# Layer norms that measure from a first mean over half of the chunks, in a two-layer Conformer / MLA / expert trunk

## What is computed

```python
def layer_norm(x, g, b):
    mu = jnp.mean(xf, -1, keepdims=True)
    var = jnp.mean(jnp.square(xf - mu), -1, keepdims=True)
    return ((xf - mu) * lax.rsqrt(var + LN_EPS) * g + b).astype(x.dtype)

# norm 0, inside the convolution mixer
y = jax.nn.silu(layer_norm(conv, g_ln, b_ln)) @ w_out
# norms 1 and 3 (mixer), norm 2 (SwiGLU of layer 0)
xp = layer_norm(ALPHA * xp + mp, ln_g[i, 0], ln_b[i, 0])
xp = layer_norm(ALPHA * xp + fp, ln_g[i, 1], ln_b[i, 1])
```

## Time and profile before

| | |
|---|---|
| median of 3 runs | 1913.56 us (1909.77 to 1916.96) |
| profiled execution | 1914.0 us, of which the span is 1912.4 us |
| mean granted TensorE clock | 0.957 |
| busy | TensorE 91%, weight loads 78%, VectorE 73%, ScalarE 58%, GpSimd 5% |
| moved | 460.86 MB, 241 GB/s over the span |

### The profile page before, as it was taken

The page is one execution under the profiler, slowest core; times in us unless marked ns, Lnnn a source line. Parts: engine busy times, 40 slices in busy tenths (PEclk is TensorE's granted clock), DMA queues, the critical chain, the costliest instruction groups (busy, mean ns, idle before and its releaser), DMA issues.

```text
span 1912.4 us, 27003 instructions
## 1 busy us (share of the span) xinstructions
PE 1748.3 (91%) x9480; PEld 1492.9 (78%) x9480; DVE 1388.5 (73%) x1494; ACT 1104.1 (58%) x1144; POOL 86.4 (5%) x174
## 2 busy tenths in 40 slices
PE   6998899998888998779999999989999999999990
PEld 5987899997757887757888888768888888888880
DVE  4995655436455665456888889888888888888885
ACT  4434543226254454136777777667777777777771
POOL 0000000000013441010000000000000000000001
PEclk9999999999889998959999999999999999999995
DMA  9653454443111441047999999989999999999963
GB/s 236 206 183 94 111 154 148 138 121 131 37 52 55 130 117 48 2 152 266 347 348 356 346 358 352 340 337 372 370 376 380 371 371 361 393 370 372 383 246 111
DMA packets 229126, 460.86 MB, mean 241 GB/s; under 512 B 16533, under 2 KB 121652, under 8 KB 229025
## 3 DMA queue, kind: packets, MB, share of 16 engines
q1 hardware_dynamic: 217438, 433.76, 63.5%
q10 hardware_dynamic: 6067, 18.86, 2.8%
q0 software_dynamic: 5536, 7.12, 1.4%
HBM read 441.40 MB, written 18.76 MB: 241 GB/s over the span
## 4 chain that ended last, share of the span: by engine, by line
issue 54%; PE 38%; DVE 4%; ACT 2%; DMA 1%; POOL 1%; SPq 0%; POOLq 0%; ACTq 0%; DVEq 0%
PE ps L1859 7%; PE ps L1861 7%; PE ps L1860 7%; PE ps L2200 3%; PE ps L1924 3%; PE ps L2169 2%; PE ps L1964 1%; PE ps L1957 1%; PE ps L2219 1%; PE ps L2195 1%; PE ps L2220 1%; DMA xtok<-in_x_sample 1%; PE ps L2279 1%; PE ps L2054 0%; DVE rstd L1349 0%
## 5 line engine op out<-in xcount | busy, mean ns | idle before, releaser
L1764 DVE TENSOR_TENSOR w_lo<-raw,w_hi 128x2048 fp32r<-128x2048 f32 x212 | 484.0, 2291 | 82.9 <-ACT w_hi L1145 82.9
L1145 ACT ACTIVATE w_hi<-raw 128x2048 fp32r<-128x2048 f32 x212 | 406.1, 1919 | 161.8 <-PE ps L2407 151.8
L1773 DVE TENSOR_TENSOR w_lo<-raw,f_hi 128x2048 fp32r<-128x2048 f32 x126 | 284.0, 2285 | 27.2 <-PE ps L2311 17.4
L1154 ACT ACTIVATE f_hi<-raw 128x2048 fp32r<-128x2048 f32 x126 | 237.3, 1913 | 70.6 <-PE ps L2311 47.9
L1859 PE MATMUL ps<-x_hi,w_hi 128*128 128x304 f32 x672 | 210.2, 313 | 25.1 <-DVE x_lo L1355 15.0
L2405 PE MATMUL ps<-w_hi,g_hi 128*128 128x512 f32 x560 | 220.1, 393 | 3.3 <-DVE w_lo L1764 3.3
L2407 PE MATMUL ps<-w_hi,g_lo 128*128 128x512 f32 x560 | 218.2, 390 | 0.0
L2406 PE MATMUL ps<-w_lo,g_hi 128*128 128x512 f32 x560 | 218.0, 389 | 0.0
L1861 PE MATMUL ps<-x_lo,w_hi 128*128 128x304 f32 x672 | 206.6, 307 | 0.0
L1860 PE MATMUL ps<-x_hi,w_lo 128*128 128x304 f32 x672 | 206.1, 307 | 0.0
L1274 DVE TENSOR_TENSOR w_lo<-raw,w_hi 128x2048 fp32r<-128x2048 f32 (+4 forms) x129 | 135.5, 1096 | 83.4 <-ACT w_hi L884 83.3
(11 more groups left out here) (412 smaller groups left out, 3107.9 us busy)
## 6 DMA issues: line engine op xcount, KB each, us to landing
raw<-in_moe_w_gu SPq DMA_DIRECT2D x224, 1024.0 KB, 7.1
raw<-in_moe_w_down SPq DMA_DIRECT2D x112, 1024.0 KB, 7.0
raw<-in_ffn_w_gu SPq DMA_DIRECT2D x44, 512.0 KB, 5.0
kvn<-in_cache_ckv SPq DMA_DIRECT2D x128, 128.0 KB, 2.4
raw<-in_conv_w_in SPq DMA_DIRECT2D x16, 512.0 KB, 8.3
raw<-in_ffn_w_down SPq DMA_DIRECT2D x16, 512.0 KB, 4.0
rows_in<-zrow ACTq DMA_DIRECT2D x13, 512.0 KB, 4.9
raw<-in_conv_w_out SPq DMA_DIRECT2D x8, 512.0 KB, 6.7
```

The costliest lines, as they stand in the source:

```text
L1145: nc.scalar.activation(w_hi[:, u % SPLIT], raw[:, u % RAW], ACT.Copy).then_inc(hi_done, 1)
L1154: nc.scalar.activation(first_hi(k), first_raw(k), ACT.Copy).then_inc(hi_done, 1)
L1764: V.tensor_tensor(w_lo[:, u % SPLIT], raw[:, u % RAW], w_hi[:, u % SPLIT].bitcast(F32), ALU.subtract).then_inc(lo_done, 1)
L1773: V.tensor_tensor(w_lo[:, (U_MOE + k) % SPLIT], first_raw(k), first_hi(k).bitcast(F32), ALU.subtract).then_inc(lo_done, 1)
```

## The change

All four norms are made in another way. When half of the chunks are there (0 to 3), their mean is taken as a first mean, and all chunks are stored as distances from it. Squares are taken of these distances. At the end the sum of the distances gives the shift to the true mean (`ln_delta`), and the variance is the mean square minus the shift's square. Each chunk is then re-centred by the shift before it is scaled. So the squares of six chunks are made before the last product has ended.

- VectorE, second to fourth norm (`norm_sums`): after the first and second residual it adds chunks 0 to 3 into `rstd`. After the third it reads the first mean, subtracts it from chunks 0 to 5, adds chunks 4 and 5 into `rstd`, and adds squares 0 to 3 into `sq[:, 0]`. After the fourth residual it subtracts from chunks 6 and 7. Each residual ends with a wait for itself.
- TensorE (`shift_and_spread`): no `mean_terms` between products; one sum after the third product for the first mean; after the fourth, four sums of what VectorE prepared, then chunks 6 and 7 of the mean, then squares 6 and 7.
- ScalarE: six squares after the splits (in the third norm ahead of the split of unit 9 of 12), two at the end; the root reads `rstd` from SBUF, where VectorE has put the variance.
- First norm: four sums of chunks 0 to 3 stand between the convolution's products; VectorE subtracts from chunks 0 to 5 ahead of the last `add_taps`; TensorE makes eight sums after the last taps and the rest as above. The convolution's product groups alternate between two pairs of PSUM banks in place of three. The edge rows are turned after the variance; VectorE copies them after the norm and one split, and ScalarE issues their nine transfers behind two splits.
- GpSimd's `iota` into `place_no` waits for the last scaling of the fourth norm instead of the last product.

```diff
+    HALF_MEAN = 2.0 / D
+    ln_m0 = [rstd[:], gate[:, 0], ln_rows[:, DC - 3], xt[:, 0, 0:T]]
+    ln_banks = [(4, 5), (6, 7), (6, 7), (6, 7)]
...
-        pool.wait_ge(unit_used, U_MOE)
+        pool.wait_ge(ln_scaled, DC * 4)
...
+        def squares(n, chunks):
+
+            for c in chunks:
                 act.wait_ge(ln_cent, DC * n + c + 1)
...
+        def root(n):
+
+            squares(n, (DC - 2, DC - 1))
+            act.wait_ge(ln_ready, ln_base(n + 1))
+            nc.scalar.activation(rstd[:], rstd[:], ACT.Sqrt, bias=eps[:, 0:1]).then_inc(ln_std, 1)
...
         for i in range(12):
+            if i == 9:
+                squares(2, range(DC - 2))
             split(U_DOWN + i + AHEAD)
...
         settle()
+        first_mean(0)
+        distance(0, range(DC - 2))
         add_taps(7)
...
+            def center(c):
+
+                mark(V.tensor_tensor(work[:, c], work[:, c], ln_delta, ALU.subtract))
+                at[c] = n_own[0]
+
+            v.wait_ge(ln_mean, 2 * n + 2)
+            chain(V.tensor_scalar(ln_delta, ps[:, mean_at, 0:T], 1.0 / D, None, ALU.mult))
+            mark(V.tensor_tensor(ln_dsq, ln_delta, ln_delta, ALU.mult))
+            squared = n_own[0]
+            center(0)
+            v.wait_ge(dve, squared)
+            v.wait_ge(ln_var, n + 1)
+            V.scalar_tensor_tensor(out=rstd[:], in0=ps[:, var_at, 0:T], scalar=1.0 / D, in1=ln_dsq,
+                                   op0=ALU.mult, op1=ALU.subtract).then_inc(ln_ready, 1)
+            center(1)
             v.wait_ge(ln_std, n + 1)
             chain(V.reciprocal(rstd[:], rstd[:]))
             for c in range(DC + 2):
                 if c < DC:
+                    v.wait_ge(dve, at[c])
                     V.tensor_tensor(work[:, c], work[:, c], rstd[:], ALU.mult).then_inc(ln_scaled, 1)
+                    if c + 2 < DC:
+                        center(c + 2)
...
+        def norm_sums(n, i):
+
+            if i == 0:
+                mark(V.tensor_tensor(rstd[:], work[:, 0], work[:, 1], ALU.add))
+            elif i == 1:
+                settle()
+                chain(V.tensor_tensor(rstd[:], rstd[:], work[:, 2], ALU.add))
+                V.tensor_tensor(rstd[:], rstd[:], work[:, 3], ALU.add).then_inc(ln_ready, 1)
+            elif i == 2:
+                first_mean(n)
+                distance(n, range(DC - 2))
+                v.wait_ge(ln_cent, DC * n + DC - 2)
+                V.tensor_tensor(rstd[:], work[:, 4], work[:, 5], ALU.add).then_inc(ln_ready, 1)
+                v.wait_ge(ln_sq, DC * n + 2)
+                mark(V.tensor_tensor(sq[:, 0], sq[:, 0], sq[:, 1], ALU.add))
+                v.wait_ge(ln_sq, DC * n + 4)
+                chain(V.tensor_tensor(sq[:, 2], sq[:, 2], sq[:, 3], ALU.add))
+                V.tensor_tensor(sq[:, 0], sq[:, 0], sq[:, 2], ALU.add).then_inc(ln_ready, 1)
...
+            if 3 <= m_ <= 6:
+                pe.wait_ge(ln_ready, m_ - 2)
+                m = sum_up(ln_banks[0][0], work[:, m_ - 3], m_ == 3, m_ == 6)
+        m.then_inc(ln_mean, 1)
...
+        def shift_and_spread(n, before):
+
+            mean_at, var_at = ln_banks[n]
+            for bank, src, first in before:
+                sum_up(bank, src, first, False)
+            for c in (DC - 2, DC - 1):
+                pe.wait_ge(ln_cent, DC * n + c + 1)
+                m = sum_up(mean_at, work[:, c], False, c == DC - 1)
+            m.then_inc(ln_mean, 1)
+            for c in (DC - 2, DC - 1):
                 pe.wait_ge(ln_sq, DC * n + c + 1)
+                m = sum_up(var_at, ln_sq_of[n][:, c], False, c == DC - 1)
             m.then_inc(ln_var, 1)
...
-                if i >= 1:
-                    pe.wait_ge(group_free, g0 + i)
-                    mean_terms(2 * i - 2, 2)
-            pe.wait_ge(group_free, g0 + 4)
-            mean_terms(DC - 2, 2, signal=True)
-            spread(n)
+                if i == 2:
+                    if n == 1:
+                        pe.wait_ge(edge_copied, 1)
+                    pe.wait_ge(ln_ready, ln_base(n) + 1)
+                    sum_up(mean_at, rstd[:], True, True).then_inc(ln_mean, 1)
+            pe.wait_ge(ln_ready, ln_base(n) + 3)
+            pe.wait_ge(ln_sq, DC * n + DC - 2)
+            shift_and_spread(n, [(var_at, sq[:, 0], True), (mean_at, rstd[:], True),
+                                 (var_at, sq[:, 4], False), (var_at, sq[:, 5], False)])
```

More of the change, by code:

```diff
@@ L943, in layer_norm @@
                 nc.scalar.activation(x_hi[:, c], work[:, c], func, scale=g(c), bias=b(c)).then_inc(ln_hi, 1)
+        squares(0, range(DC - 2))
         act.wait_ge(y_st, ZERO_STORES * 16)
         layer_norm(0, sq, ACT.Silu, lambda c: cg[:, c:c + 1], lambda c: cb[:, c:c + 1])
-        act.wait_ge(edge_copied, 1)
-        act.dma_start(new_conv_p[0, 0], edge[0:HIST, 0]).then_inc(edge_out, 16)
-        for s_ in range(DEC_B):
-            act.dma_start(new_conv_s[0, s_, HIST - DEC_T:HIST], edge[DEC_T * s_:DEC_T * s_ + DEC_T, 1]).then_inc(edge_out, 16)
         for i in range(4):
             split(U_COUT + i + AHEAD)
+            if i == 1:
+                act.wait_ge(edge_copied, 1)
+                act.dma_start(new_conv_p[0, 0], edge[HALF:HALF + HIST, 0]).then_inc(edge_out, 16)
+                for s_ in range(DEC_B):
+                    act.dma_start(new_conv_s[0, s_, HIST - DEC_T:HIST], edge[DEC_T * s_:DEC_T * s_ + DEC_T, 1]).then_inc(edge_out, 16)
+        squares(1, range(DC - 2))
         layer_norm(1, xres, ACT.Identity, lambda c: lng[:, 0, c:c + 1], lambda c: lnb[:, 0, c:c + 1])
@@ L1106, in _ @@
             split(U_MOUT + i + AHEAD)
-        spread(3)
+        squares(3, range(DC - 2))
+        root(3)
         for c in range(DC):
@@ L1304, in add_taps, with first_mean, distance @@
             chain(V.reduce_sum(work[:, m, T_P:T], prod.rearrange("p s t k -> p (s t) k"), AX))
+            V.tensor_scalar(work[:, m, T_P:T], work[:, m, T_P:T], b_dw[:, m:m + 1], None, ALU.add)
             v.wait_ge(diag_used, PE_TAPS * (m + 1))
-            V.tensor_tensor(wp, wp, ps[:, 6 + m % 2, 0:T_P], ALU.add).then_inc(ln_in, 1)
-            V.tensor_scalar(work[:, m, T_P:T], work[:, m, T_P:T], b_dw[:, m:m + 1], None, ALU.add)
+            V.tensor_tensor(wp, wp, ps[:, 6 + m % 2, 0:T_P], ALU.add).then_inc(ln_ready, 1)
+        def first_mean(n):
+            v.wait_ge(ln_mean, 2 * n + 1)
+            chain(V.tensor_scalar(ln_m0[n], ps[:, ln_banks[n][0], 0:T], HALF_MEAN, None, ALU.mult))
+        def distance(n, chunks):
+            for c in chunks:
+                V.tensor_tensor(work[:, c], work[:, c], ln_m0[n], ALU.subtract).then_inc(ln_cent, 1)
         for m in range(8):
@@ L1334, in _ @@
         settle()
+        first_mean(0)
+        distance(0, range(DC - 2))
         add_taps(7)
[L1336 to L1340 removed]
+        settle()
+        v.wait_ge(ln_ready, DC)
+        distance(0, (DC - 2, DC - 1))
+        V.tensor_copy(u_new[:].rearrange("p c (s t) -> p c s t", s=DEC_B), u_s[:, :, :, HIST:]).then_inc(ln_ready, 1)
         def layer_norm(n, out, split_x=True):
[L1344 to L1347 removed]
+            mean_at, var_at = ln_banks[n]
+            at = {}
+            def center(c):
[11 more added lines that the diff above has]
+            center(1)
             v.wait_ge(ln_std, n + 1)
@@ L1866, in linear @@
             pe.wait_ge(lo_done, off + (u + 1))
-            if first and g >= 3 and free:
-                pe.wait_ge(group_free, off + (g - 2))
+            if first and g >= 2 and free:
+                pe.wait_ge(group_free, off + (g - 1 if g < G_COUT else g - 2))
             hi, lo = layout(w_hi[:, u % SPLIT]), layout(w_lo[:, u % SPLIT])
@@ L1901, in _, with sum_up @@
         nc.tensor.transpose(ps[:, 2, 0:VEC_ROWS], vrow[0:VEC_ROWS], ident[0:VEC_ROWS, 0:VEC_ROWS]).then_inc(vec_turned, 1)
+        def sum_up(bank, src, first, last):
+            return nc.tensor.matmul(ps[:, bank, 0:T], ones[:], src, start=first, stop=last, skip_group_check=True)
         def turn_history():
@@ L1952, in stats @@
                 m.then_inc(signal, 1)
-        def mean_terms(c0, n_chunks, signal=False):
-            for c in range(c0, c0 + n_chunks):
-                m = nc.tensor.matmul(ps[:, 6, 0:T], ones[:], work[:, c], start=c == 0, stop=c == DC - 1, skip_group_check=True)
-            if signal:
-                m.then_inc(ln_mean, 1)
-        def spread(n):
-            for c in range(DC):
+        def shift_and_spread(n, before):
+            mean_at, var_at = ln_banks[n]
+            for bank, src, first in before:
[5 more added lines that the diff above has]
+            for c in (DC - 2, DC - 1):
@@ new lines, in product_and_norm @@
+            pe.wait_ge(ln_sq, DC * n + DC - 2)
+            shift_and_spread(n, [(var_at, sq[:, 0], True), (mean_at, rstd[:], True),
+                                 (var_at, sq[:, 4], False), (var_at, sq[:, 5], False)])
+        pe.wait_ge(ln_cent, DC - 2)
+        pe.wait_ge(ln_sq, DC - 2)
```

(9 more changed lines are left out.)

58 lines of the change are left out of this document (28 added, 30 removed).

## The result

| | before | after |
|---|---|---|
| median | 1914.28 us (4 runs, 1909.77 to 1916.96) | 1898.01 us (4 runs, 1895.89 to 1899.72) |
| profiled execution, span | 1914.0, 1912.4 | 1899.7, 1898.1 |
| mean granted TensorE clock | 0.957 | 0.957 |

The ratio is 0.9917, 95% interval [0.9895, 0.9939]: 0.83% faster. The forecast was 1898.5 us.

The account below looks back on a forecast made before the run. It took TensorE, busy 91% of the span, and the norms' chain of work, which no products overlap, as the bound. Gains of 2.5, 4.0, 4.2 and 4.8 us, together 15.5 off 1914.0, gave 1898.5 us; eight in ten, 1892 to 1907.

Parts of the forecast that it names:

- Last residual to first scaling: Second to fourth norm: from start of last residual to start of first scaling 7.51 us instead of 10.79, gain 3.28.
- The late residual of the second norm: Second norm: VectorE's queued work makes the last residual 0.65 us late; 0.2 charged, bounds 0 and 0.65.
- Sums between products: Norms two to four: one chunk sum between products instead of two pairs, gain 1.53 us per norm.
- Later first product: First three norms: re-centrings queue ahead of the low halves, so the next product starts 0.6 us later after first scaling.
- First norm: End of the convolution stage: first scaling at 150.9 instead of 154.00 us, gain 3.1, less 0.6 for the later product.
- The sign given for it, 126.6: Convolution stage: the profile would show VectorE's last gate at 126.6 us; it started at 125.13 before.
- Fourth norm and routing: Fourth norm: gain 3.28+1.53, 4.8 us; re-centrings hide behind the router's 48 matmuls of 9.75 us.
- Rival (b): Norms: VectorE becomes the bound and its added operations (17 each in norms two to four) are paid, 1922 us; chance 0.04.
- Rival (c): Last residual 2 us late in norms two and three, first norm gives nothing: 1905 us; chance 0.15.
- Rival (a): TensorE's clock after norm gaps: longer half-clock spells, 1903.5 us, chance 0.15; or clock up in routing, 1891.5, chance 0.07.

Follow-up runs that it names:

- the fillers: Changed kernel plus f32 matmuls that nobody reads on TensorE in the gaps of all four norms; 1888.83 us (ratio 0.9864), again 1888.38 us (0.9877).
- third norm alone: Changed kernel plus matmuls that nobody reads on TensorE in the third norm's gap only; 1894.56 us, ratio 0.9909.

## Why the prediction was right

- **Last residual to first scaling** (forecast 7.51 us): 804.41 - 796.88 = 7.53 in the fourth norm, 428.62 - 421.10 = 7.52 in the third, 190.62 - 183.44 = 7.18 in the second, where the residual itself is late.
- **The late residual of the second norm** (0.65 late, 0.2 charged): 0.56 late. From the end of the last product 3.09 us are won, the sum had 3.28 - 0.2 = 3.08.
- **Sums between products** (1.53 per norm): together with the former and the 0.6 back, first to second reciprocal was to shrink by 4.0 and second to third by 4.2; measured 4.16 and 4.16. Putting all sums back on TensorE costs by the means what they were priced at, 10.6 us against 10.7.
- **Later first product** (0.6, charged in full): it starts 0.61 later after the first scaling, and the first low half 2.32 after it, as worked out. Whether all of it is paid hangs on the clock: first to second reciprocal is 39.55 with a spell of 3 us behind the first norm and 39.1 at full clock.
- **First norm** (3.1): right. The column of the table says 2.92, but it holds a start that differs by 1.2 us among executions; counted from the first gate the gain is 3.0 to 3.1. Of the 0.6 charged behind it 0.45 shows. VectorE started on the last gate at 127.32, 2.19 later than before, where four sums were to make 2.04. The sign given for it, 126.6, did not fit the prediction's own sum, 125.13 + 2.04 = 127.17, and did not come.
- **Fourth norm and routing** (4.8): nothing of the re-centrings shows. The router's 48 products take 9.75 us as before; the router's result came 14.6 us earlier than before where 15.5 was summed. The missing 0.8 lies between third and fourth reciprocal. Half of it stands right behind the third norm: from its reciprocal to the next one it takes 38.56 us where it took 37.54, at the same mean level of 0.91, so 1.0 was given back where 0.6 was charged. Why 1.0 no run shows, and the remaining 0.4 has no cause either; this stretch has anything from 369.1 to 375.8 us in kernels with nearly the same work.
- **Rival (b)** is refuted: a load on VectorE beyond the change's is paid in full where VectorE is behind (second norm) and not at all where it waits (third). Its count was a little low: each of the norms two to four has 18 operations more, not 17, and with the 11 of the first they are the 65 by which VectorE's records grew (1494 to 1559). They made 25.6 busy us, not 31.7. **Rival (c)**, two microseconds late and no gain in the first norm, did not come about either: 0.56, 0 and 0 late, 3.0 won in the first norm.
- **Rival (a)** did not happen in the profiled execution (mean clock 0.957 both times). Its premise is right and larger than I had it: with all sums on TensorE the two groups of executions lie 8 us apart. The changed kernel's 15 executions span 1891.1 to 1901.2, those of before 1908.7 to 1917.0. The Trainium skill, "TensorE: Matmul & The Clock Gate", section on what is actually happening, says that the moment of release varies from run to run; the first norm's gap, left behind at 1.00, for 3 us at 0.50 or for 6 us at 0.50, agrees.
- **Luck.** The sum of 15.5 us lies between 14.3, the difference of the two profiled executions, and 16.3, that of the medians. The terms are shown one by one, within 0.8 us each; that the median came within 0.5 us of 1898.5 is luck, as executions of one kernel differ by 8 to 10 us.

Of the 9 to 12 us of the fillers some 5.4 are theirs by the columns: 0.5 behind the first norm (39.09 against 39.55, though a kernel without them was at full clock there too), 0.8 behind the second (235.40 against 236.24), 2.2 behind the third and 1.9 in routing. That is the 5 us of the theory. The rest stands where the spells come and go: some 1.7 us between second and third reciprocal, and 4.0 to 4.5 in the attention stage (373.59 with the third norm's fillers alone against 369.09 and 369.57), where kernels without a filler ahead of it got nearly as far (370.38 and 370.58, with the spell behind the third norm in it). Whether all fillers together make these stretches rarer stays open, and so does why the executions of one build keep to one or two sets of spells (the eight of the kernel kept busy lie within 1887.4 to 1892.4).

## What to carry to other kernels

Where a reduction ends a stage, take from behind the last product all that can be made from what is there already: distances from a provisional mean allow the squares of six of eight chunks, and pair sums on an idle VectorE spare a busy TensorE 0.51 us each. Price it by the distance between two markers of the chain, and look at the residual's bracket to see whether the helper engine still waits; once it has no bracket, each microsecond more is paid, and perhaps twice through the clock. Before timing differences of less than 0.5%, cut several traces of the same kernel at the same markers, the first of them behind the loads of the start: only what repeats in a column belongs to the edit.

## What the runs showed of the hardware

- The same wait of TensorE for `h_lo`, 1.88 us in the middle of the SwiGLU stage, is followed by about 3 us at half clock in eight of the fourteen traces (0.55 in the window of the changed kernel) and by none in six (1.00 in "third norm alone").
- Work that nobody reads, 5.6 us of it in a gap, kept the level at 1.00 behind the second norm in three of three traces and behind the third in four of four; without it the level was 0.50 there in every trace. The next product started no later after the first low half, 0.61 us with it and 0.62 without.
- Filling the fourth norm's gap did not make the router's products twice as fast: 7.94 instead of 9.75 us. The window from 800 to 810 us of the kernel with fillers in routing alone has a mean level of 0.76, so the level falls again while these small products run:

```profile
800.00:810.00 10.00, 9.00 (x54) 8.16 (x52) 6.52 (x15) 5.01 (x8) 0.77 (x4) 0.76 0.00 0
```
